# A longer filler for the delta rule's waits, new homes for two low halves, and a shorter gate product

## The reference, cut to what matters

```python
proj = rmsnorm(x) @ w_in            # includes the gate columns a and bt, 6 each
y_pool = pool_mixer(u_pool, ...)    # 512 channels  (tiles 0 to 3 of the mixed activations)
y_gdn  = gated_deltanet(q, k, v, z, a, bt, ...)   # 768 channels (tiles 4 to 9), six heads of 128
y_lru  = rglru_mixer(xr, gr, ...)   # 768 channels (tiles 10 to 15)
x = x + concatenate([y_pool, y_gdn, y_lru]) @ w_out        # w_out is 2048 x 2048
x = x + conv_ffn(rmsnorm(x), ...)
```

## Time and profile before

| what | us |
|---|---|
| median of 3 runs | 2094.57 (2091.99 to 2094.84) |
| the profiled execution | 2092.1, span 2090.1 |
| TensorE busy | 2071.5 of the span |
| VectorE / ScalarE / GpSimd busy | 1313.8 / 961.8 / 129.4 |
| the middle, first gram product to chunk 2 of the out projection | 1137.59 to 1205.27 |

### The profile page before, as it was taken

How to read it: one execution, slowest core, us unless ns; L and a number is a source line. 1 busy time by engine, 2 the same in 40 slices (tenths; PEclk the granted TensorE clock), 3 DMA queues, 4 the chain that set the end, 5 groups by cost and what they waited for, 6 DMA issues and landing times.

```text
span 2090.1 us, 28025 instructions
## 1 busy us (share of the span) xinstructions
PE 2071.5 (99%) x11271; PEld 1796.3 (86%) x11271; DVE 1313.8 (63%) x1400; ACT 961.8 (46%) x1013; POOL 129.4 (6%) x83
## 2 busy tenths in 40 slices
PE   9999999999999999999999999999999999999998
PEld 8888888888888888888888878888888888888887
DVE  6666656565556557567788655776546764467655
ACT  6444445444444446544667344355333443343433
POOL 0000000000011000030001100012100121000210
PEclk9999999999999999999999999999999999999999
DMA  9755555666656657545554145556565555555553
GB/s 343 241 182 182 181 163 189 195 182 190 189 174 187 186 170 249 194 152 175 168 183 153 41 154 197 193 183 195 188 200 183 192 190 191 191 189 194 182 200 121
DMA packets 318029, 387.36 MB, mean 185 GB/s; under 512 B 9354, under 2 KB 251483, under 8 KB 317659
## 3 DMA queue, kind: packets, MB, share of 16 engines
q1 hardware_dynamic: 309499, 373.93, 55.6%
q10 hardware_dynamic: 8416, 11.78, 1.6%
HBM read 383.58 MB, written 4.69 MB: 186 GB/s over the span
## 4 chain that ended last, share of the span: by engine, by line
PE 97%; DVE 2%; ACT 1%; issue 0%; DMA 0%; DVEq 0%; ACTq 0%
PE acc L1796 39%; PE acc L1806 21%; PE acc L1859 8%; PE acc L1854 8%; PE acc L1855 8%; PE acc L1769 2%; PE acc L1768 2%; PE acc L1773 2%; PE aux L1961 1%; PE aux L1987 1%; PE aux L1972 1%; PE aux L1887 1%; PE aux L2182 0%; PE acc L1737 0%; PE acc L1741 0%
## 5 line engine op out<-in xcount | busy, mean ns | idle before, releaser
L957 DVE TENSOR_TENSOR w_lo<-raw,w_hi 128x2048 fp32r<-128x2048 f32 x343 | 795.2, 2319 | 540.2 <-ACT w_hi L465 539.6
L465 ACT ACTIVATE w_hi<-raw 128x2048 fp32r<-128x2048 f32 (+2 forms) x351 | 663.2, 1890 | 668.5 <-PE acc L1806 313.7
L1796 PE MATMUL acc<-act_x,w_hi 128*128 128x512 f32 x2112 | 510.9, 394 | 0.3 <-ACT w_hi L465 0.3
L1796 PEld LDWEIGHTS acc<-act_x,w_hi 128*128 128x128 f32 x2112 | 390.2, 188 | 77.4 <-issue 0.4
L1796 PE MATMUL acc<-ff_x,w_hi 128*128 128x512 f32 x1536 | 366.6, 391 | 0.0
L1796 PEld LDWEIGHTS acc<-ff_x,w_hi 128*128 128x128 f32 x1536 | 282.4, 188 | 54.7
L1806 PEld LDWEIGHTS acc<-act_x,w_lo 128*128 128x128 f32 x2112 | 270.6, 191 | 10.0
L1806 PE MATMUL acc<-act_x,w_lo 128*128 128x256 f32 x2112 | 274.7, 283 | 0.0
L1806 PEld LDWEIGHTS acc<-ff_x,w_lo 128*128 128x128 f32 x1536 | 196.9, 191 | 7.5
L1806 PE MATMUL acc<-ff_x,w_lo 128*128 128x256 f32 x1536 | 199.4, 283 | 0.0
L1854 PE MATMUL acc<-w_hi,act_x 128*128 128x512 f32 x464 | 181.9, 392 | 2.7 <-DVE act_x L1448 2.7
(11 more groups left out here) (334 smaller groups left out, 1773.9 us busy)
## 6 DMA issues: line engine op xcount, KB each, us to landing
raw<-in_ffn_up SPq DMA_DIRECT2D x96, 1024.0 KB, 5.1
raw<-in_w_in_c SPq DMA_DIRECT2D x64, 1024.0 KB, 5.7
raw<-in_w_in_ab SPq DMA_DIRECT2D x49, 1024.0 KB, 5.1
raw<-in_ffn_down SPq DMA_DIRECT2D x48, 1024.0 KB, 5.0
raw<-in_w_in SPq DMA_DIRECT2D x40, 1024.0 KB, 5.3
raw<-in_w_out_ab SPq DMA_DIRECT2D x16, 1024.0 KB, 5.1
raw<-in_w_out_c SPq DMA_DIRECT2D x16, 1024.0 KB, 5.2
raw<-in_w_out SPq DMA_DIRECT2D x16, 1024.0 KB, 5.0
```

What stands on the lines that cost most here:

```text
L465: copy = lambda out, in_, **k: nc.scalar.activation(out, in_, ACT.Copy, **k)
L957: tt(w_lo[:, c % 2], raw[:, c], w_hi[:, c % 2].bitcast(F32), ALU.subtract).then_inc(lo_ready, 1)
L1796: mm(out(j), wide(w_hi[:, c % 2])[:, k, j * P:(j + 1) * P], x[:, 8 * r + k, :, :].rearrange("p a s -> p (a s)"), start=(r == 0 and k == 0) ...
```

## The change

- **Pieces.** Panels 0 and 1 of the out projection are worked through in eight pieces `OUT2_PIECES`, each a (panel, chunk): chunks 0 and 1 of panel 0, then of panel 1, then chunks 2 and 3 of both. The first four pieces, 24 parts, are threaded into the middle. Panel 0 is added to the residual stream after piece 5, panel 1 after piece 7. SyncE's loads follow the new order. PSUM homes move (`u_bank`, `norm_bank`, `x_bank`, `v_bank`), since panel 1 holds `acc[:, 1]`.
- **GpSimd** makes the LRU's low half: tiles 2 to 5 after the three pack masks, tiles 0 and 1 after the first round's masks.
- **VectorE** makes the low half of piece 2's weights in two halves, within the first and second round (`half_split`), that of piece 3 after the second u, and of pieces 4 and 5 after the last `low_part`. ScalarE rounds piece 2 between the value copies, piece 3 after the rounds, piece 4 between the root and the gated outputs' rounding, piece 5 last.
- **Gates.** High and low gate weights lie side by side (24 columns); one matmul with the high activations writes 24 rows, one with the low activations adds to 12 of them. The two transposes become two products with `fold_gates`, a stacked pair of identities, which also add the halves. VectorE builds that matrix by one addition.

```diff
+OUT2_PIECES = ((0, 0), (0, 1), (1, 0), (1, 1), (0, 2), (0, 3), (1, 2), (1, 3))
-        u_bank, carry_bank = acc[:, 1, :], aux[:, 0:2, :].rearrange("p b n -> p (b n)")
-        norm_bank = lambda j: aux[:, 3, :] if j == 2 else acc[:, 1, j * PANEL:(j + 1) * PANEL]
+        u_bank, carry_bank = (aux[:, b:b + 2, :].rearrange("p b n -> p (b n)") for b in (2, 0))
+        norm_bank = lambda j: aux[:, (3, 0, 1)[j], :]
...
# ScalarE, middle()
-                for g in range(3):
-                    beta_values(g)
+                beta_values(0)
+                beta_values(1)
+                split(AT_OUT2, 2)
+                beta_values(2)
...
-                split(AT_OUT2, 2)
+                split(AT_OUT2, 3)
                 for j in range(3):
                     act.wait_ge(go_ready, j + 1)
...
                 f(go_norm, go_norm, ACT.Sqrt, bias=eps).then_inc(go_root, 1)
+                split(AT_OUT2 + 1, 0)
                 for j in range(3):
                     act.wait_ge(go_y, j + 1)
                     copy(act_hi[:, POOL_G + 2 * j:POOL_G + 2 * j + 2, :], tiles(K0 + 2 * j, 2)).then_inc(mid_hi, 1)
+                split(AT_OUT2 + 1, 1)
# VectorE, middle()
-                better(FIRST_ROUND, amid=lambda: low_of(tiles(XR0, LRU_B), POOL_G + GDN_H, LRU_B))
-                for r in range(FIRST_ROUND + 1, 4):
+                better(FIRST_ROUND, amid=lambda: half_split(2, 0))
+                better(FIRST_ROUND + 1, amid=lambda: half_split(2, 2).then_inc(lo_ready, 1))
+                for r in range(FIRST_ROUND + 2, 4):
                     better(r)
...
-                split(AT_OUT2, 2)
+                split(AT_OUT2, 3)
...
                 low_part(2)
+                split(AT_OUT2 + 1, 0)
+                split(AT_OUT2 + 1, 1)
# GpSimd
             pack_mask(1)
             pack_mask(2)
+            pool.wait_ge(mid_hi, 2)
+            lru_low(2, LRU_B)
             for r in range(FIRST_ROUND, 5):
...
+                if r == FIRST_ROUND:
+                    lru_low(0, 2)
# TensorE, gates
-                        mm(aux[0:12, 0, 0:S], w_h, act_hi[:, k, :], start=(k == 0), stop=False)
-                        mm(aux[0:12, 0, 0:S], w_h, act_lo[:, k, :], start=False, stop=False)
-                        ins = mm(aux[0:12, 0, 0:S], w_l, act_hi[:, k, :], start=False, stop=(k == NK - 1))
+                        mm(aux[0:24, 0, 0:S], gw[:, k, :], act_hi[:, k, :], start=(k == 0), stop=False,
+                           skip_group_check=True)
+                        ins = mm(aux[0:12, 0, 0:S], gw_hi[:, k, :], act_lo[:, k, :], start=False, stop=(k == NK - 1),
+                                 skip_group_check=True)
# TensorE, middle()
                 pe.wait_ge(evacuated, 2 * AT_OUT2 - 1)
+                out_parts(0, 0, 4)
                 pe.wait_ge(silu_done, 4)
+                pe.wait_ge(gram_masked, GDN_H)
                 turn_values(0)
                 turn_values(1)
-                pe.wait_ge(gram_masked, GDN_H)
+                out_parts(0, 4, 6)
                 pe.wait_ge(packed_rows, 3)
...
                 turn_values(2)
+                out_parts(1, 0, 3)
                 pe.wait_ge(gv_ready, 2)
-                for part in range(4):
-                    out_part(0, part)
                 for g in range(3):
                     turn_inverse(g)
...
-                out_part(0, 4)
-                out_part(0, 5)
+                out_parts(1, 3, 6)
...                                        # u
-                out_part(1, 0)
+                out_parts(2, 0, 1)
...                                        # carry
-                out_part(1, 1)
+                out_parts(2, 1, 3)
...                                        # u again
-                out_part(1, 2)
+                out_parts(2, 3, 4)
...                                        # o
-                for part in range(3, 6):
-                    out_part(1, part)
+                out_parts(2, 4, 6)
+                out_parts(3, 0, 2)
                 for j in range(3):
                     pe.wait_ge(go_scaled, j + 1)
...
+                out_parts(3, 2, 6)
+            def out2():
+                for at in range(4, 7):
+                    out_parts(at, 0, 6)
+                turn_summed(3, AT_OUT2, 0)
+                out_parts(7, 0, 6)
+                deproject(AT_OUT2, N_OUT, act_hi, act_lo, between=turning(3, AT_OUT2), order=OUT2_ORDER, first=2)
```

More of the change, by code:

```diff
@@ L552, in between @@
                             also(i, c)
-                    out_panel(gp0 + i, between, last=last and i == N_OUT - 1, begun=begun and i == 0)
+                    out_panel(gp0 + i, between, last=last and i == N_OUT - 1, begun=0 if i else begun)
                 if x_hi is not None:
@@ L976, in panel, with out_panel @@
                         between(c)
-            def out_panel(gp, out, between=None, last=False, begun=False, before=None):
+            def out_panel(gp, out, between=None, last=False, begun=0, before=None):
                 for c in range(4):
@@ L985, in out_panel @@
                         out()
[L986 to L988 removed]
+                    if c < begun:
+                        pass
+                    elif c < 2:
+                        split(gp, c + 2)
                     elif not last:
@@ L1085, in low_of_x, with out_panels, before @@
                 ins.then_inc(lo_act, 1)
-            def out_panels(k, gp0, out, gain, x_hi, x_lo, begun=False):
-                for i in range(N_OUT):
+            def out_panels(k, gp0, out, gain, x_hi, x_lo, paired_up=False):
+                for i in range(1 if paired_up else 0, N_OUT):
+                    def before(c):
+                        if c == 1 and i == 1 and paired_up:
+                            dve.wait_ge(w_used, 4 * (gp0 + 1) + 2)
+                            out(0)
                     def between(c):
@@ L1092, in between @@
                             low_of_x(k, i - 1, gain, x_hi, x_lo)
-                    out_panel(gp0 + i, lambda: out(i), between, begun=begun and i == 0)
+                    out_panel(gp0 + i, lambda: out(i), between, before=before)
                 low_of_x(k, N_OUT - 1, gain, x_hi, x_lo)
@@ L1832, in out_part, with out_parts, deproject @@
                         for t in range(NT):
-                            ins = mm(out(t), x(act_hi, k, t), w_lo[:, c, k, :], start=False, stop=False)
+                            ins = mm(out(t), x(act_hi, k, t), w_lo[:, at % 2, k, :], start=False,
+                                     stop=(c == 3 and k == QK - 1))
                 if part == 5:
                     ins.then_inc(w_used, 1)
-            def deproject(gp0, n, hi, lo, ready=None, between=None, order=range(4), begun=0):
-                for i in range(n):
+            def out_parts(at, first, end):
+                for part in range(first, end):
+                    out_part(at, part)
+            def deproject(gp0, n, hi, lo, ready=None, between=None, order=range(4), first=0):
+                for i in range(first, n):
                     gp = gp0 + i
-                    if not (begun and i == 0):
-                        pe.wait_ge(evacuated, 2 * gp - 1 if i == 0 else 2 * gp - 2)
+                    pe.wait_ge(evacuated, 2 * gp - 1 if i == 0 else 2 * gp - 2)
                     out = lambda t: acc[:, i % 2, t * PANEL:(t + 1) * PANEL]
-                    for c in range(begun if i == 0 else 0, 4):
+                    for c in range(4):
                         if between:
```

95 lines of the change are left out of this document (52 added, 43 removed).

## The result

The changed kernel takes 2079.97 us (median of 6 runs, 2079.76 to 2080.08); the kernel before took 2091.90 (6 runs, 2091.05 to 2094.84). The ratio is 0.9939, interval 0.9927 to 0.9952: faster by 0.6%, clear of noise, 11.9 us between the medians. The profiled executions are 2092.1 and 2079.76 us, their spans 2090.1 and 2077.7: 12.4 us between them.

The account below looks back on a forecast made before the run. TensorE, busy 99%, was taken as the bound, with 11.9 us lost in the middle. 11.0 - 2.6 + 1.7 + 1.7 - 0.4 = 11.4 us off 2092.1 gave 2080.7, plus 2.5 made 2083.2 us; range 2080.0 to 2087.5.

Parts of the forecast that it names:

- The price of filler: Out projection parts in the middle: 48 more matmuls ahead of piece 4, 0.229 us apart, 11.0 us of work done early.
- The first stage: Up to the rounds: spread products without wait but 1.7 us late; unpacking 4.0 us after them, before GpSimd's hold-up.
- GpSimd against VectorE: Block inversion: moved GpSimd work holds up VectorE's two-input steps, 1.3 us; a rival without this, 12%, was 1.3 us faster.
- The rounds at no cost: First two rounds: VectorE's half subtractions, 1.2 us each, fit in at cost 0, at most 2 x 1.2.
- The tail: From the rounds to piece 4: filler covers the waits of 0.81, 0.74 and 2.65 us; piece 4 starts 2.6 us late.
- The gates: Gate product: 16 fewer matmuls save 1.8 us, the two folding products cost 0.1, net 1.7 us.
- The sum: Whole kernel: filler less delay, plus clock and gates, less 0.4 for operand changes, makes 11.4 us gained.
- the last one: Final step: 2080.7 us from the profiled execution, plus 2.5 because the median shown lies above it, makes 2083.2 us.
- The clock fall before the first round: Rival, 22%: TensorE doing only transposes and nothing for 3.3 us drops the clock, costing 1.7 us: 2084.9.
- The gate rival: Gate product: 24 output rows cost what two matmuls did, so 1.7 us less gain, 2084.9; chance 6%.
- the slower one: Rival, 3%: the rounds run at half clock, their short products not raising it, 22 us more: 2105.
- the delta rule's chain: Rival, 12%: chain lengthened by a round's half subtraction (1.2 us) or piece 4's rounding (0.8); with both 2085.2.

Follow-up runs that it names:

- The twelve-part run: Changed kernel with pieces 2 and 3 run whole behind the output transposes, leaving 12 parts in the middle instead of 24: 2088.66 us.
- the unread matmuls' run: Kernel before, with matmuls whose result nobody reads put into its two long waits (22 and 18): 2088.86 us, ratio 0.9985.
- the cover: Changed kernel with the three parts ahead of the inverse's first transposes put behind the rounds: 2084.20 us.
- the kernel with the first wait filled: Kernel before with 22 unread matmuls in the 3.9 us wait before the spread products alone: 2090.46 us, ratio 0.9996.

## Why the prediction was right or wrong

**The bound and the two waits: right.** Both went, and with them both falls of the clock.

**The price of filler, 11.0 us: right** (10.9). The twelve-part run shows it from the other side.

**The first stage: right in place.** The spread products were 1.4 us late (forecast 1.7). From their start to the unpacking 5.18 us passed, where 4.0 + 1.3 had been summed; the 4.0 is borne out by the unread matmuls' run (0.62 us to the first step here, 3.42 from it there).

**GpSimd against VectorE: right, mechanism and size.** 0.42 us in the first step and 0.71 in the second, 1.1 us against 1.3 expected; the wait it leaves is 1.1 us. I expected the transposes behind the wait to be spaced by the unpacking as well, with 2.0 us idle in all; they were spaced by only 0.3 us. TensorE's idle time in the middle was thus 1.8 us (1.4 in the stretches above, 0.4 in the gram products) and not the 3.7 forecast: 0.9 less here and 0.9 less in the tail.

**The rounds at no cost: right.** TensorE is busy 24.00 of 24 us, with half a subtraction (1.22 us each) in two of them.

**The tail: sized 0.7 us too late.** The filler met each wait as written: the output transposes begin without one. The delay was 1.9, not 2.6: by the table 0.3 of that was gained in the first stage, 0.2 behind the rounds and 0.2 in the last parts. The 0.4 us put into the sum for more changes between operand kinds was not needed on top. ScalarE's rounding of piece 4 made nothing late: by the time line of VectorE the low half that the piece waits for was there at about 1204.7, 0.9 us before the piece began, where 1.1 had been forecast.

**The gates: 1.7 forecast, 1.44 and 1.36 measured.** The two folding products of 24 rows cost 0.32 us, not 0.1.

**The sum: 11.4 forecast, 12.4 between the profiles, 11.9 between the medians.** The 1.0 us between the first two is 0.7 of delay, 0.4 of operand changes, the 0.18 unexplained and 0.05 of the clock, less 0.26 for the gates and 0.1 for the filler.

**The step that failed is the last one**: "the median shown is 2.5 above it, so 2083.2", and with it the range's lower end. That offset is 2.5 of the 3.2 us by which the forecast missed; the rest is the sum's, 0.7 us too small against the median. I carried an offset of three runs (two of them at 2094.6 to 2094.8) over to a kernel that does not have it. Over all 58 runs of the kernel before the sets' medians are 2091.5 to 2091.9, and only five runs are above 2092.2. With the profiled execution's own 2092.1 as base the same sum gives 2080.7, against 2079.97 measured. That the time lies just outside the range and not just inside is chance, since the changed kernel's own runs spread over 0.3 us; the offset is not. What the runs showed in its place: the kernel before's time varies by up to 4.6 us, and with its two idle stretches filled by 0.34 us, because those stretches drop the clock for a varying time (none, 3.4 or 6.8 us fit the runs seen). A change that fills the waits takes the long runs away with them. The runs at 2094.6 were not profiled. But the record has a mean clock for 52 of the 58 runs: 0.996 for the two at 2094.6 and 0.997 or 0.998 for the others, so longer falls in these two are likely. The run at 2093.74 has 0.998, and the clock does not explain it.

**The rivals.** The clock fall before the first round did not come, with 1.1 us idle and 1.7 us of transposes there; at 3.9 us idle it did. The gate rival is refuted by 32 matmuls in 3.71 us, the slower one by the clock's return within the first round once the cover was taken away. GpSimd and VectorE did meet, and the delta rule's chain got no longer: from u to the transposes it takes 16.33 us in the kernel before, in the changed kernel and without the eight parts.

## What to carry to other kernels

Where an engine is 99% busy, list its waits, and price a wait with the clock that follows it: here 3.9 and 2.65 us of idle time cost another 2.85 us through the clock. Filler whose operands are ready early was worth its whole length here (10.9 us for 48 matmuls), less what it delayed, and the order of the helpers' queues behind it is worth a look: GpSimd work beside VectorE's short two-input steps stretched them by 1.1 us, and moving one of its instructions gave 0.6 us back. Forecast against the profiled execution or many runs; an offset of three runs of a kernel that idles may be its own clock.

## What was not expected of the hardware

- The same wait of 2.65 us came with 3.4 us at 1.2 GHz in the kernel before and with 6.8 us in the kernel with the first wait filled, and in two of that kernel's runs, by their times and mean clocks, with none. The five kernels without long waits repeat within 0.2 to 0.8 us, those with them within 1.1 to 4.6.
- A float32 matmul with 24 contraction rows and 12 columns costs 0.27 us in a pair that interrupts rounded products, against 0.11 for a transpose of 12 rows in the same place.
